# Expert outputs of a routed mixture: accumulating scatters onto a copy of h in DRAM in place of scattered pair rows that TensorE adds

## What is computed

```python
def _hier_moe(x, ...):
    p1 = jax.nn.softmax((x @ w_r1).astype(jnp.float32) + b_r1, axis=-1)
    v1, g_sel = lax.top_k(p1, 1)
    ...
    v2, e_idx = lax.top_k(l2_sel, TOP_K_INNER)
    w2 = jax.nn.softmax(v2, axis=-1)
    ...
    for g in range(N_EXPERT_GROUPS):
        hg = jnp.einsum('nd,edf->nef', x, w_gate[g])
        hu = jnp.einsum('nd,edf->nef', x, w_up[g])
        a = jax.nn.silu(hg) * hu * gate[:, g, :, None]
        y = y + jnp.einsum('nef,efd->nd', a, w_down[g])
    return y

h1 = layer_norm(DN_ALPHA * x + mix, ln1_g, ln1_b)
f = _hier_moe(h1, ...)
return layer_norm(DN_ALPHA * h1 + f, ln2_g, ln2_b)
```

## Time and profile before

| | us |
|---|---|
| median of three executions | 1029.32 |
| the profiled execution, its time | 1036.87 |
| its span | 1035.0 |
| TensorE busy | 911.5 (88%) |
| VectorE busy | 553.9 (54%) |
| ScalarE busy | 409.9 (40%) |
| GpSimd busy | 177.8 (17%) |

### The profile page before, as it was taken

How to read it: one execution, slowest core, us unless ns; L and a number is a source line. 1 busy time by engine, 2 the same in 40 slices (tenths; PEclk the granted TensorE clock), 3 DMA queues, 4 the chain that set the end, 5 groups by cost and what they waited for, 6 DMA issues and landing times.

```text
span 1035.0 us, 13339 instructions
## 1 busy us (share of the span) xinstructions
PE 911.5 (88%) x5132; PEld 642.8 (62%) x5132; DVE 553.9 (54%) x1023; ACT 409.9 (40%) x748; POOL 177.8 (17%) x82
## 2 busy tenths in 40 slices
PE   6999999968999999669999439999999989999585
PEld 6999879944555555458887336666656555665231
DVE  5202020067657565855444576666666666675157
ACT  5202020034554555642222135555546445554045
POOL 0000000320000000000000011545454444453100
PEclk9999999998999999999999668999999999999888
DMA  9999998298777476257420836999999998994374
GB/s 345 323 358 364 362 335 327 87 348 282 253 272 275 159 261 235 82 190 282 165 82 26 333 139 226 349 350 346 358 334 339 311 328 320 354 362 138 142 259 171
DMA packets 54847, 273.49 MB, mean 264 GB/s; under 512 B 13984, under 2 KB 16544, under 8 KB 39680
## 3 DMA queue, kind: packets, MB, share of 16 engines
q1 hardware_dynamic: 46016, 247.97, 67.1%
q0 software_dynamic: 8768, 24.66, 6.8%
HBM read 256.33 MB, written 95.30 MB: 340 GB/s over the span
## 4 chain that ended last, share of the span: by engine, by line
PE 60%; DMA 14%; DVE 10%; ACT 6%; issue 5%; POOL 5%; SPq 0%; POOLq 0%; DVEq 0%; ACTq 0%
PE psum L645 54%; DMA back<-h_d,back 11%; POOL pair_d L1656 5%; PE psum L704 3%; ACT gu_high L1086 3%; PE psum L883 2%; DMA back<-pair_d 1%; DVE back L1231 1%; ACT back L490 1%; DVE back L1213 1%; DVE stats L1216 1%; PE psum L843 1%; ACT back L995 1%; ACT front L1106 1%; DMA middle<-pair_d 1%
## 5 line engine op out<-in xcount | busy, mean ns | idle before, releaser
L1656 POOL DMA_INDIRECT pair_d<-front,back x32 | 127.2, 3976 | 177.6 <-ACT front L1106 127.6
L645 PE MATMUL psum<-back,front 128*64 128x128 f32 (+1 forms) x896 | 149.8, 358 | 5.9 <-ACT back L490 4.4
L645 PEld LDWEIGHTS psum<-back,front 128*64 128x64 f32 (+1 forms) x896 | 70.4, 147 | 62.0 <-issue 52.4
L645 PE MATMUL psum<-gu_high,xg_high 128*112 128x512 f32 x256 | 104.1, 407 | 2.1 <-DVE xg_low L1481 2.1
L645 PE MATMUL psum<-front 64*128 64x256 f32 (+5 forms) x384 | 93.2, 497 | 10.8 <-DVE stats L1213 10.5
L645 PE MATMUL psum<-gu_high,xg_low 128*112 128x512 f32 x256 | 101.8, 398 | 0.0
L645 PE MATMUL psum<-gu_low,xg_high 128*112 128x512 f32 x256 | 101.5, 397 | 0.0
L645 PE MATMUL psum<-x_high,w_high 128*128 128x352 f32 x288 | 94.0, 327 | 8.3 <-DVE w_low L361 8.3
L645 PE MATMUL psum<-x_low,w_high 128*128 128x352 f32 x288 | 93.3, 324 | 0.0
L645 PE MATMUL psum<-x_high,w_low 128*128 128x352 f32 x288 | 93.2, 324 | 0.0
L490 ACT COPY back<-psum 128x512 f32<-128x512 f32 (+1 forms) x88 | 46.9, 547 | 84.9 <-PE psum L704 84.8
(11 more groups left out here) (198 smaller groups left out, 1712.0 us busy)
## 6 DMA issues: line engine op xcount, KB each, us to landing
out_win_k_s<-cache_win_k SPq DMA_DIRECT2D x16, 2044.0 KB, 13.6
out_win_v_s<-cache_win_v SPq DMA_DIRECT2D x16, 2044.0 KB, 12.8
back<-w_down SPq DMA_DIRECT2D x24, 1024.0 KB, 7.6
front<-w_gu SPq DMA_DIRECT2D x22, 1024.0 KB, 6.9
middle<-w_gu SPq DMA_DIRECT2D x22, 1024.0 KB, 7.7
back<-w_gu SPq DMA_DIRECT2D x20, 1024.0 KB, 7.4
back<-winkT SPq DMA_DIRECT2D x8, 1792.0 KB, 8.8
back<-cache_win_v SPq DMA_DIRECT2D x8, 1024.0 KB, 6.9
```

The costliest lines, as they stand in the source:

```text
L645: return nc.tensor.matmul(out, lhsT, rhs, start=start, stop=stop, skip_group_check=True)
L1656: G.indirect_dma_start(pair_d, bass.IndirectOffsetOnAxis(ap=IDX[0:CAP, NE + e:NE + e + 1], axis=0), YS[e % 2][0:CAP, :], None, bounds_chec ...
```

## The change

Five edits, together.

1. `pair_d` goes. A new DRAM tensor `sum_d` with one row per token takes its place. When a chunk of h is stored to `h1_d`, it is stored to `sum_d` as well.
2. The scatter of an expert's result goes to the token's row of `sum_d` with `compute_op=ALU.add`: the DMA adds to what stands there. The first one waits until all nine stores of the copy have landed.
3. The experts are worked in the order `TURN`: 0, 8, 16, 24, 1, 9, ..., one of each group in turn. Tokens of different groups are different, so two scatters in flight at once never add to the same row. Weights, lists and scales are picked by `TURN[e]`; buffers and semaphores go by e as before.
4. Routing drops the column of pair numbers (three columns become two) and divides the weights by alpha, since the rows now hold h + f / alpha. The norm makes up for it by alpha squared in the variance and a factor alpha on gamma.
5. In the tail the nine chunks of `sum_d` are loaded, 512 KB each, into nine buffers `RF[c]`, all issued at once; TensorE's additions and VectorE's L1590 go, as do the waits on three buffers. ScalarE's and VectorE's norm is as before.

```diff
+TURN = [(n % NG) * EPG + n // NG for n in range(NE)]
...
-        pair_d = nc.dram_tensor("pair_d", [NPAIR, D], F32, kind="Internal").ap()
+        sum_d = nc.dram_tensor("sum_d", [TOK, D], F32, kind="Internal").ap()
...
-        YP = [at(off, 2, D) for off in (24720, 27024, 29072)]
-        RF = [at(18576 + D * s, D) for s in range(3)]
+        RF = [at(18576 + D * c, D) for c in range(8)] + [at(27024, D)]
...
         def load_gu(sp, e, half):
             k = slice(4 * half, 4 * half + 4)
-            sp.dma_start(GUF[e % 3][:, k, :], I["w_gu"][e][:, k, :]).then_inc(s_gf[e % 3][half], 16)
+            sp.dma_start(GUF[e % 3][:, k, :], I["w_gu"][TURN[e]][:, k, :]).then_inc(s_gf[e % 3][half], 16)
         def load_dn(sp, e):
-            sp.dma_start(WD[e % 4], I["w_down"][e]).then_inc(s_wd[e % 4], 16)
+            sp.dma_start(WD[e % 4], I["w_down"][TURN[e]]).then_inc(s_wd[e % 4], 16)
         R0 = 13600 + 324
...
             def store_h1(c):
                 sp.wait_ge(s_h1, c + 1)
                 sp.dma_start(h1_d[c * P:c * P + rows(c), :], H1[0:rows(c), c, :]).then_inc(s_h1d, 16)
+                sp.dma_start(sum_d[c * P:c * P + rows(c), :], H1[0:rows(c), c, :]).then_inc(s_init, 16)
             for c in range(CH):
                 if c >= 2:
...
             sp.wait_ge(s_ys[0], 16 * (NE // 2))
             sp.wait_ge(s_ys[1], 16 * (NE // 2))
-            pr = pair_d.rearrange("(k n) d -> n k d", k=2)
-
-            def store_y(c):
+            for c in range(CH):
+                sp.dma_start(RF[c][0:rows(c), :], sum_d[c * P:c * P + rows(c), :]).then_inc(s_sum2[c], 16)
+            for c in range(CH):
                 sp.wait_ge(s_fo, c + 1)
-                sp.dma_start(O["y"][c * P:c * P + rows(c), :], RF[c % 3][0:rows(c), :]).then_inc(s_out[c % 3], 16)
-
-            for c in range(CH):
-                if c == 0:
-                    sp.wait_ge(s_y, NE)
-                if c >= 3:
-                    sp.wait_ge(s_ysum, c - 2)
-                sp.dma_start(YP[c % 3][0:rows(c), :, :], pr[c * P:c * P + rows(c), :, :]).then_inc(s_yp[c % 3], 16)
-                if c >= 3:
-                    store_y(c - 3)
-            for c in range(CH - 3, CH):
-                store_y(c)
-            for i in range(3):
-                sp.wait_ge(s_out[i], 16 * (CH // 3))
+                sp.dma_start(O["y"][c * P:c * P + rows(c), :], RF[c][0:rows(c), :]).then_inc(s_out, 16)
+            sp.wait_ge(s_out, 16 * CH)
             for i in range(2):
                 sp.wait_ge(s_copy[i], 16 * DB * 2)
...
             with pe.Else():
                 pe.nop()
-            pe.wait_ge(s_ya, NE)
-            pe.wait_ge(s_yd, NE)
-            for c in range(CH):
-                m = rows(c)
-                pe.wait_ge(s_yp[c % 3], 16 * (c // 3 + 1))
-                if c >= 2:
-                    pe.wait_ge(s_f1, c - 1)
-                for n in range(2):
-                    o = PS[0:m, 1024 * (c % 2) + 512 * n:1024 * (c % 2) + 512 * n + 512]
-                    mm(o, ident[0:m, 0:m], YP[c % 3][0:m, 0, 512 * n:512 * n + 512], True, False)
-                    last = mm(o, ident[0:m, 0:m], YP[c % 3][0:m, 1, 512 * n:512 * n + 512], False, True)
-                last.then_inc(s_ysum, 1)
-
         @block.scalar
         def _(act):
...
             for c in range(CH):
                 m = rows(c)
-                r, mu, sq, std = RF[c % 3][0:m, :], MV2[0:m, c, 0:1], MV2[0:m, c, 1:2], MV2[0:m, c, 2:3]
-                act.wait_ge(s_f1, c + 1)
+                r, mu, sq, std = RF[c][0:m, :], MV2[0:m, c, 0:1], MV2[0:m, c, 1:2], MV2[0:m, c, 2:3]
+                act.wait_ge(s_sum2[c], 16)
                 if c:
                     act.wait_ge(s_sq2, c)
                 nc.scalar.activation(SPARE[0:m, :], r, ACT.Identity, scale=-1.0 / D, accum_out=mu).then_inc(s_mean2, 1)
                 act.wait_ge(s_mean2, c + 1)
                 nc.scalar.activation(SPARE[0:m, :], r, ACT.Square, bias=mu, accum_out=sq).then_inc(s_sq2, 1)
                 act.wait_ge(s_sq2, c + 1)
-                nc.scalar.activation(std, sq, ACT.Sqrt, scale=1.0 / D, bias=EPSC[0:m, :]).then_inc(s_std2, 1)
+                nc.scalar.activation(std, sq, ACT.Sqrt, scale=ALPHA ** 2 / D, bias=EPSC[0:m, :]).then_inc(s_std2, 1)
         @block.vector
...
             dve.wait_ge(s_ra, 2)
             step(V_.tensor_scalar(v1, W2, 1.0, None, ALU.add))
             step(V_.reciprocal(v1, v1))
-            step(V_.tensor_tensor(v1, v1, p1, ALU.mult))
+            step(V_.scalar_tensor_tensor(v1, v1, 1.0 / ALPHA, p1, ALU.mult, ALU.mult))
             step(V_.tensor_tensor(v2, v1, W2, ALU.mult))
             for k in range(2):
                 step(V_.tensor_tensor(RV[:, k, :, 0:NE], RE[k], wide(tok1, NE), ALU.mult))
-                step(V_.scalar_tensor_tensor(RV[:, k, :, NE:2 * NE], RE[k], float(k * TOK), RV[:, k, :, 0:NE], ALU.mult, ALU.add))
-                step(V_.tensor_tensor(RV[:, k, :, 2 * NE:3 * NE], RE[k], wide((v1, v2)[k], NE), ALU.mult))
+                step(V_.tensor_tensor(RV[:, k, :, NE:2 * NE], RE[k], wide((v1, v2)[k], NE), ALU.mult))
             dve.wait_ge(s_rank, 1)
             for k in range(2):
                 step(V_.tensor_tensor(RX, RE[k], bank(0)[:, 0:CH * NE].rearrange("p (c e) -> p c e", c=CH), ALU.mult))
...
-            dve.wait_ge(s_y, NE)
+            dve.wait_ge(s_gb2, 32)
+            step(V_.tensor_scalar(GB2[:, 0, :], GB2[:, 0, :], ALPHA, None, ALU.mult))
             for c in range(CH):
-                m = rows(c)
-                dve.wait_ge(s_ysum, c + 1)
-                if c >= 3:
-                    dve.wait_ge(s_out[c % 3], 16 * (c // 3))
-                V_.scalar_tensor_tensor(RF[c % 3][0:m, :], H1[0:m, c, :], ALPHA, PS[0:m, 1024 * (c % 2):1024 * (c % 2) + 1024],
-                                        ALU.mult, ALU.add).then_inc(s_f1, 1)
-                if c:
-                    normalised(c - 1)
-            normalised(CH - 1)
+                normalised(c)
         @block.gpsimd
...
                 pool.wait_ge(sem_, count)
                 pool.sem_inc(s_past, 1)
-            last_token, last_pair = pool.to_reg(TOK - 1), pool.to_reg(NPAIR - 1)
+            last_token = pool.to_reg(TOK - 1)
             def gather(e):
-                G.indirect_dma_start(XG[e % 2][0:CAP, :], None, h1_d, bass.IndirectOffsetOnAxis(ap=IDX[0:CAP, e:e + 1], axis=0),
+                G.indirect_dma_start(XG[e % 2][0:CAP, :], None, h1_d, bass.IndirectOffsetOnAxis(ap=IDX[0:CAP, TURN[e]:TURN[e] + 1], axis=0),
                                      bounds_check=last_token, oob_is_err=False).then_inc(s_gx[e % 2], 16)
             def scatter(e):
-                G.indirect_dma_start(pair_d, bass.IndirectOffsetOnAxis(ap=IDX[0:CAP, NE + e:NE + e + 1], axis=0), YS[e % 2][0:CAP, :], None,
-                                     bounds_check=last_pair, oob_is_err=False).then_inc(s_ys[e % 2], 16)
+                G.indirect_dma_start(sum_d, bass.IndirectOffsetOnAxis(ap=IDX[0:CAP, TURN[e]:TURN[e] + 1], axis=0), YS[e % 2][0:CAP, :], None,
+                                     bounds_check=last_token, oob_is_err=False, compute_op=ALU.add).then_inc(s_ys[e % 2], 16)
+
+            def added(e):
+                if e == 0:
+                    pool.wait_ge(s_init, 16 * CH)
+                pool.wait_ge(s_ya, e + 1)
+                await_(s_yd, e + 1)
+                scatter(e)
             await_(s_idx, 1)
             gather(0)
...
-                    pool.wait_ge(s_ya, e)
-                    await_(s_yd, e)
-                    scatter(e - 1)
-            pool.wait_ge(s_ya, NE)
-            await_(s_yd, NE)
-            scatter(NE - 1)
+                    added(e - 1)
+            added(NE - 1)
             with overflow(pool):
```

More of the change, by code:

```diff
@@ L230, in build @@
         OPOS, OVAL = at(15872 + 512, 2, CH), at(15872 + 530, 2, CH, 4)
-        OLF, OLI = at(16500, 4), at(16504, 2).bitcast(U32)
+        OLF, OLI = at(16500, 4), at(16504, 1).bitcast(U32)
         OPRE = [at(16510, NE), at(16542, NE)]
@@ L268, in build @@
         s_gb2 = sem("s_gb2")
[L269 to L272, removed]
+        s_init, s_zero = sem("s_init"), sem("s_zero")
+        s_sum2 = [sem(f"s_sum2_{c}") for c in range(CH)]
+        s_mean2, s_sq2, s_std2, s_fo, s_out = (sem(n) for n in ("s_mean2", "s_sq2", "s_std2", "s_fo", "s_out"))
         o_pos, o_eb, o_oh, o_ohx, o_idx = (sem(n) for n in ("o_pos", "o_eb", "o_oh", "o_ohx", "o_idx"))
@@ L479, in build @@
         RX = at(R0 + 1440, CH, NE)
-        RV = at(9216, 2, CH, 96)
+        RV = at(9216, 2, CH, 2 * NE)
         OH = [at(50832 + P * s, P) for s in range(4)]
-        IDX = at(34960, 3 * NE).bitcast(U32)
-        IDF = at(35056, 3 * NE)
+        IDX = at(34960, NE).bitcast(U32)
+        IDF = at(35056, 2 * NE)
         def transposed_out(eng, copy, n):
@@ L494, in build @@
         W2 = G1W[:, 0:CH]
-        GS = IDF[:, 2 * NE:3 * NE]
+        GS = IDF[:, NE:2 * NE]
         @block.sync
@@ L871, in _ @@
                 pe.wait_ge(s_oh, n + 1)
```

(26 more changed lines are left out.)

11 lines of the change are left out of this document (5 added, 6 removed).

## The result

The changed kernel takes 1047.62 us, the median of four executions (1041.93 to 1050.15), against 1029.27 for the kernel before in the same comparison. The ratio is 1.0123, with a 95% interval of 1.0073 to 1.0174: somewhat slower, inside the 2% that was called no change. With the executions that came beside the experiments, the kernel before has medians from 1032.7 to 1033.6, so 1.2 to 1.4% is the better figure than the 18 us between the first medians. (The ratio and its interval come from comparing the executions; they need not equal the quotient of two medians, here 1.018.)

What follows compares the result with a forecast made beforehand. The prediction took a two-expert chain of scatter issue, gather flight and ScalarE's rounding and scaling as the bound. From the median 1029.3, tail -21.6, routing -1.7 and adding scatter +27 gave +3.7, forecast 1033, range 1009 to 1064.

Steps and rivals of the forecast that it cites:

- What bounds the kernel now: Expert loop: a two-expert chain of scatter issue, gather flight and ScalarE's rounding and scaling sets the pace, 10.79 us per expert.
- The rival of full DMA engines: Expert loop: DMA engines, not the chain, become the bound; +24 to +34, time 1030 to 1040; chance 0.16.
- The tail, -21.6: After the last scatter: identity matmuls, VectorE's L1590 and half of every load go, 21.6 us less.
- five steps: Tail: landing 5.0, load 4.0, ScalarE to first std 4.0, VectorE 24.4 for nine chunks, store and end 2.5.
- Routing, -1.7: Routing: two VectorE operations of 0.49 each go and the one-hot product narrows, 1.7 us less.
- the product gets a third narrower, 0.7: Routing: the one-hot product's 36 matmul passes, 6.13 us for 96 columns, narrow by a third, taken as 0.7 saved.
- The copy of h and the order, 0 each: Before and in the loop: nine more stores of h are hidden, and the new expert order changes no loads; 0 each.
- The adding scatter, +27: Expert loop: the addition lengthens the following gather's flight by 2.0, once per two experts, 27 us more.
- X: Expert loop: what a gather's flight gains from the adding scatter ahead of it; between 0 and 5.9, taken as 2.0.
- The scatters' issue keeps its 4.25: Expert loop, GpSimd: issuing an adding scatter takes 4.25 us as before, since VectorE's four L1476 still stand beside it.
- nearly free: Expert loop: the addition lengthens gather flight by up to 0.5; loop +0 to +7, time 1006 to 1013; chance 0.22.
- The second read queues on its own: Expert loop: gather flight gains 4 to 5.9; loop +54 to +80, time 1060 to 1086; chance 0.20.

Runs made afterwards that it cites:

- a_plain_delay2: Changed kernel with plain scatters and a GpSimd memset of 4096 columns between each scatter and the gather behind it: 1052.5 us, ratio 1.0224.
- a_early: Changed kernel with the gather of expert e+2 issued right after the transposes of e, ahead of the scatter of e-2: 1025.2 us, ratio 0.9929.
- b_early: Kernel before with plain scatters and the gather of expert e+2 issued right after the transposes of e: 1021.1 us, ratio 0.99.
- b_turn: Kernel before with only the experts' order changed, one of each group in turn: 1035.5 us, ratio 1.0039.
- a_plain: Changed kernel with plain scatters in place of adding ones, sums left out, output not usable: 1008.4 us, ratio 0.9799.
- a_plain_early: Changed kernel with plain scatters, sums left out, and gathers issued ahead of earlier scatters: 997.7 us, ratio 0.9617.
- b_early_deep: Kernel before with early gathers and nine buffers for pair rows, all nine tail loads issued at once, TensorE still adding: 1016.0 us, ratio 0.9788.

## Why the prediction was right, and where it was not

The forecast was 1033 with a range from 1009 to 1064; 1047.6 lies inside, and the class, within 2%, is the one that was held likeliest.

*What bounds the kernel now*: right. The chain of scatter, gather and rounding sets the pace in this order of issue (a_plain_delay2), and the DMA engines' time is the bound just behind it (a_early; in b_early TensorE is full as well). The rival of full DMA engines was wrong for the changed kernel and right for a_early.

*The tail, -21.6*: -21.3. Four of five steps were within 0.6; the landing was 5.7 in place of 5.0, which the load's 3.5 in place of 4.0 all but made up.

*Routing, -1.7*: +0.35 against the profile of before, -0.2 against b_turn. The two operations of VectorE are gone (0.98), but the step "the product gets a third narrower, 0.7" had the wrong sign: the product ran at the lower clock throughout, 7.94 us against 6.13 (6.67 in b_turn).

*The copy of h and the order, 0 each*: right (b_turn; the first gather lies between 615.2 and 619.7 in all traces, whatever the edit). The +4.1 ahead of the loop belongs to the spread of executions: 3.7 of it stood at the first store of h, in code that isn't changed.

*The adding scatter, +27*: between the two profiles +28.0, but the profile of before held a long loop; against a_plain it is 33, and in the timed executions, together with the tail's landing, 33 to 39. So the +28.0 is nearer to +27 by luck than by the sum. The term's mechanism, a later gather on the chain, was right and its size short, with faults that partly cancel. X was taken as 2.0; the flight gained 1.5 in the median and 1.2 in the mean. "The scatters' issue keeps its 4.25" was wrong: 0.54 more, from GpSimd's own work, since the idle issue grew by as much. TensorE's clock after long waits is nowhere in the text, which has only more long stalls, and those in a rival; the slower `down` matmuls make 0.37 per expert, about 10 us if they lie on the path. And the base was low: the median of before was 1029.3 in three executions and near 1033 in more. The last two and the routing (10, 4 and 2 us) are about as large as the 15 us between 1033 and the measured time.

*The DMA engines' time behind X* was split wrongly. The text priced the weights at 411 GB/s, 7.65 us per expert, which left 1.3 each for a gather and a scatter. In the window of before from the fifth gather to the 31st, the weights' queue has 80.7% of 280.87 us, 8.7 per expert, and the queue of gathers and scatters 13.9%, 0.75 for each of them.

*The rivals*: "nearly free" fell with a_plain. "The second read queues on its own" (X of 4 to 5.9) fell too: the flight gained 1.2 to 1.5, and the scatter's 0.76 us of engine time about doubled, with no second queueing.

## What to carry to other kernels

Here the accumulating scatter saved a load and an addition at the end, and paid with about twice its DMA engine time and, worse, with the delay of the gather in the same queue behind it. Look for a gather behind such a scatter that someone waits for, and issue that gather first; without this, a gain of 21 us in the tail cost 33 in the loop. And see whether the gain needs the new operation at all: more buffers and an earlier gather gave -18 to -19 us by the medians with plain scatters.

## What the runs showed of the hardware

- An indirect scatter of up to 112 rows of 4 KB (66 on average) that adds to DRAM, at the end of the loop: 5.5 to 6.1 us to landing against 3.6, issue 1.46 against 0.94 on GpSimd, and 1.68 us of the 16 engines' time against 0.77. In the loop it takes 0.65 us of engine time more than a plain one.
- A scatter's issue takes 4.25 where VectorE's float32 subtractions (L1476, in the changed kernel L1448) run beside it for 3.6 us, and 0.97 (the median in a_plain_early and b_early_deep) where the order moved it elsewhere. In between it grows with the overlap: 2.84 with 2.1 us of it in a_plain_early.
- Issuing an indirect gather 1.8 us later made its flight 1.6 us shorter: its arrival was set by what stood ahead of it. Issued 3.5 us later, its flight was 2.4 shorter and it arrived 1.2 later.
- A matmul series with fewer columns (64 in place of 96) took longer, 7.94 us against 7.10 in the same kernel and 6.1 to 6.7 in those of before, at a granted clock of 0.50 against 0.61 to 0.66.
